# A weight tile's remainder on VectorE instead of GpSimd, in the attention stretches of layers two and three

## What is computed

```python
for i in range(DEPTH_2):
    h = rms_norm_2(x, attn_norm[i])
    proj = h @ w_in_diff[j]            # layer two; w_in_gla[j] in layer three
    ...                                # q, k, v, mem_q from proj
    mix = diff_attention(...)          # gla_attention(...) in layer three
    cross = memory_cross_attention(mem_q, mem, mem_norm[i], w_mem_kv[i], mem_qk_norm[i])
    x = x + jnp.concatenate([mix.astype(x.dtype), cross.astype(x.dtype)], axis=-1) @ w_out[i]
    h = rms_norm_2(x, ffn_norm[i])
    x = x + conv_ffn(h, w_up[i], conv_w[i], conv_b[i], w_down[i])
```

## Time and profile before

| | us |
|---|---|
| median of 3 timed runs | 1799.42 (1798.91 to 1802.1) |
| the profiled execution | 1797.66 |
| its span, first to last instruction | 1795.9 |
| PE busy | 1735.1 (97%) |
| PE weight loads busy | 1403.9 (78%) |
| DVE busy | 945.7 (53%) |
| POOL busy | 746.8 (42%) |
| ACT busy | 477.8 (27%) |

### The profile page before, as it was taken

One profiled execution on the slowest core, in us unless ns is written; L12 is line 12 of the kernel. 1 busy time (PEld: TensorE's weight loads), 2 busy tenths in 40 slices (PEclk: granted clock), 3 DMA queues, 4 the chain that ended last, 5 costly groups with the idle time before them and its releaser, 6 DMA issues.

```text
span 1795.9 us, 28022 instructions
## 1 busy us (share of the span) xinstructions
PE 1735.1 (97%) x11634; PEld 1403.9 (78%) x11634; DVE 945.7 (53%) x1610; ACT 477.8 (27%) x1039; POOL 746.8 (42%) x372
## 2 busy tenths in 40 slices
PE   8999989999899999899999999999999999999999
PEld 7678768887667777777888888877876788888887
DVE  6676245666655376746655551234434466665311
ACT  3111123445232354423222220123121332222100
POOL 3333135200544132237555554553233665555542
PEclk9999999999899999999999999999999999999999
DMA  5222120000234122113223322221112233323332
GB/s 194 83 82 88 44 87 3 3 3 3 89 109 139 46 97 74 59 59 106 96 94 96 103 95 94 95 91 59 59 58 71 74 94 102 97 94 95 104 95 71
DMA packets 43644, 143.95 MB, mean 80 GB/s; under 512 B 5191, under 2 KB 7128, under 8 KB 43390
## 3 DMA queue, kind: packets, MB, share of 16 engines
q1 hardware_dynamic: 43518, 142.15, 24.8%
HBM read 139.50 MB, written 4.08 MB: 80 GB/s over the span
## 4 chain that ended last, share of the span: by engine, by line
PE 66%; DVE 3%; ACT 2%; issue 1%; POOL 0%; DMA 0%; DVEq 0%; SPq 0%; ACTq 0%
PE all_p_bank L214 20%; PE all_p_bank L216 19%; PE all_p_bank L215 19%; PE all_p_bank L2553 1%; PE all_p_bank L2582 1%; PE all_p_bank L2340 1%; PE all_p_bank L2316 1%; PE all_p_bank L2570 0%; PE all_p_bank L2067 0%; PE all_p_bank L3050 0%; PE all_p_bank L3032 0%; PE all_p_bank L3045 0%; PE all_p_bank L2327 0%; POOL b_wlo L195 0%; PE all_p_bank L2516 0%
## 5 line engine op out<-in xcount | busy, mean ns | idle before, releaser
L195 POOL TENSOR_TENSOR b_wlo<-b_raw,b_whi 128x1024 fp32r<-128x1024 f32 x235 | 576.2, 2455 | 748.2 <-DVE b_whi L181 745.6
L214 PE MATMUL all_p_bank<-b_hi,b_whi 128*128 128x512 f32 x1232 | 498.7, 405 | 7.7 <-issue 6.1
L216 PE MATMUL all_p_bank<-b_hi,b_wlo 128*128 128x512 f32 x1232 | 482.8, 392 | 0.0
L215 PE MATMUL all_p_bank<-b_lo,b_whi 128*128 128x512 f32 x1232 | 482.7, 392 | 0.0
L181 DVE CAST b_whi<-b_raw 128x1024 fp32r<-128x1024 f32 x238 | 184.7, 782 | 424.1 <-PE all_p_bank L216 410.3
L214 PEld LDWEIGHTS all_p_bank<-b_hi,b_whi 128*128 128x128 f32 x1232 | 233.0, 189 | 72.4 <-issue 26.1
L216 PEld LDWEIGHTS all_p_bank<-b_hi,b_wlo 128*128 128x128 f32 x1232 | 232.9, 189 | 49.9
L215 PEld LDWEIGHTS all_p_bank<-b_lo,b_whi 128*128 128x128 f32 x1232 | 233.0, 189 | 49.5 <-issue 4.1
L214 PE MATMUL all_p_bank<-f_mhi,b_whi 128*128 128x512 f32 x352 | 136.9, 389 | 0.0
L215 PE MATMUL all_p_bank<-f_mlo,b_whi 128*128 128x512 f32 x352 | 136.9, 389 | 0.0
L216 PE MATMUL all_p_bank<-f_mhi,b_wlo 128*128 128x512 f32 x352 | 136.9, 389 | 0.0
(11 more groups left out here) (459 smaller groups left out, 2566.4 us busy)
## 6 DMA issues: line engine op xcount, KB each, us to landing
b_raw<-in_w_up SPq DMA_DIRECT2D x88, 512.0 KB, 3.5
b_raw<-in_w_down SPq DMA_DIRECT2D x44, 512.0 KB, 3.5
b_raw<-in_w_in SPq DMA_DIRECT2D x32, 512.0 KB, 3.5
b_raw<-in_w_out SPq DMA_DIRECT2D x24, 512.0 KB, 3.6
b_raw<-in_w_gla SPq DMA_DIRECT2D x22, 512.0 KB, 3.5
b_raw<-in_w_diff SPq DMA_DIRECT2D x20, 512.0 KB, 3.5
b_raw<-in_w_mem SPq DMA_DIRECT2D x8, 512.0 KB, 3.6
all_x<-in_x SPq DMA_DIRECT2D x8, 256.0 KB, 5.6
```

The source lines that it names most:

```text
L195: self.nc.gpsimd.tensor_tensor(self.lo[:, n % SLOTS, :], self.raw[:, n % RAWS, :], self.hi[:, n % SLOTS, :].bitcast(F32), ALU.subtract).th ...
L214: nc.tensor.matmul(acc, lhsT=left[0], rhs=right[0], start=first, stop=False)
L215: nc.tensor.matmul(acc, lhsT=left[0], rhs=right[1], start=False, stop=False)
L216: return nc.tensor.matmul(acc, lhsT=left[1], rhs=right[0], start=False, stop=last)
```

## The change

`Ring` gets a list of tile ranges. In a range, `round` makes the remainder on DVE right behind the rounding (`low`), and `rest` on POOL skips the tile. Where a range begins, DVE waits until POOL has made the remainder of the tile in front; where one ends, POOL waits for DVE's last. The ranges are tiles 36 to 75 and 142 to 171: from the last half of layer one's output product to layer two's feed-forward, and layer three's projections and output product. In the feed-forwards POOL makes the remainders as before.

```diff
@@ Ring.__init__
+        self.ranges = []
@@ Ring.round
             self.rounded = n + 1
+            if self.whole(n):
+                if not self.whole(n - 1):
+                    dve.wait_ge(self.s_lo, n)
+                self.low(dve, n)
+
+    def whole(self, n):
+
+        return any(a <= n < b for a, b in self.ranges)
 
     def split(self, dve, n):
 
         self.round(dve, n)
+        self.low(dve, n)
+
+    def low(self, dve, n):
+
         dve.wait_ge(self.s_hi, n + 1)
         self.nc.vector.tensor_tensor(self.lo[:, n % SLOTS, :], self.raw[:, n % RAWS, :],
                                      self.hi[:, n % SLOTS, :].bitcast(F32), ALU.subtract).then_inc(self.s_lo, 1)
@@ Ring.rest
         for n in range(self.rested, min(upto + 1, len(self.tiles), self.limit)):
+            self.rested = n + 1
+            if self.whole(n):
+                continue
+            if self.whole(n - 1):
+                pool.wait_ge(self.s_lo, n)
             pool.wait_ge(self.s_hi, n + 1)
...
-            self.rested = n + 1
@@ upper_layers
+    c.ring.ranges = [(base + 4, low.ff.n_up), (low.ff.down[1].n0 + low.ff.down[1].tiles, high.ff.n_up)]
     run(nc, u.ring, base, plan + plan3, TwoLayers(low, high), Sides(*side, *side3), begin, store)
```

## The result

The changed kernel is slower: 1811.72 us, the median of 4 runs (1810.85 to 1816.08), beside 1799.78 for the kernel before on the same chip. The ratio is 1.0068, 95% interval 1.0054 to 1.0082, so +12 us where the forecast was +3.1 and the range ended at 1808. The profiled execution is the slowest of the four, 1816.08 us. In what follows a ratio is to the kernel before on the same chip, with its 95% interval in brackets; the kernel before had medians of 1799.4 to 1800.1 us on the chips used.

The account below looks back on a forecast made before the run. The prediction took TensorE (busy 1735.1 of 1795.9 us) to bound the kernel; waits added and removed at single places summed to +3.1 us, clock 0, on the timed median 1799.42, giving 1802.5 us, range 1796.5 to 1808.

Parts of the forecast that it names:

- B: Layer two, 629.7 us: two roundings ahead of the first L2641, which PE's next scores wait for; +2.4 us.
- H: Layer two, 747 us: PE's 2.99 us wait for stretched L2616 shrinks despite two remainders; net -1.6 us.
- C: Layer two, 648.9 us: one rounding ahead of L2641, L2553 starting 0.2 after it; +1.1, two like places +0.7 together.
- V: Layer three, 1376.7 us: rounding directly ahead of the last evacuation, L2809, for which PE already waits; +1.3 us.
- A: 508 us: four remainders ahead of the fourth addition to x, which L1898 on PE needs; +1.6, then -0.3 at L2032.
- L: 814 us: an unstretched rounding heads the additions PE waits for before the feed-forward; -0.6 us.
- Elsewhere idle DVE time behind the rounding takes it: Layer two's attention, other places of the L2641 pattern: idle DVE time absorbs the added remainder, so no cost was counted.
- The clash: DVE's new subtraction could be stretched by POOL's remaining work; three clashes at stalls would add 6 us, left out.
- The clock: Half-speed clock pieces behind stalls: one made, one shrunk, set against each other as 0, bounds -3.4 to +3.4 us.
- Rival 1: Layer two's attention: more stalls than counted, about nine roundings without idle DVE time behind; 1807 us, chance 0.26.
- Rival 3: All is hidden: DVE has a third of its time free, gains and costs stay off the path; 1799.5, chance 0.12.
- Rival 2: Faster: the freed interface outweighs DVE's longer queue, 629.7 and 508 us covered by other PE work; 1795.4, chance 0.14.

Follow-up runs that it names:

- e11: The change with the remainders of tiles 54 and 55 given back to POOL: 1807.33 us, ratio 1.0046 to the kernel before.
- e3: The change with eight tiles (54, 55, 57, 148, 149, 155, 167, 170) given back to POOL: 1794.89 us, ratio 0.9983 to the kernel before.
- e12: The change with the remainders of tiles 148 and 149 given back to POOL: 1805.42 us, ratio 1.0029 to the kernel before.
- e1: The change with only its first range, tiles 36 to 75 (layer two), on DVE: 1805.27 us, ratio 1.0029 to the kernel before.
- e9: The change with each DVE remainder two program steps later and ten more tiles given back to POOL, 60 left on DVE: 1793.77 us, ratio 0.9971.
- e10: The change with sixteen tiles given back to POOL, 54 left on DVE directly behind their roundings: 1793.26 us, ratio 0.9971 to the kernel before.
- e7: The change with all 70 remainders on DVE, each two program steps behind its rounding: 1800.35 us, ratio 1.0 to the kernel before.
- e6: The kernel before plus an extra DVE reduction ahead of seven roundings, its result buffer placed so no address moves: 1817.11 us, ratio 1.0100.
- e8: The change with only tile 54's remainder given back to POOL: 1814.59 us, ratio 1.0077 to the kernel before.
- e4: The kernel before plus an extra DVE reduction ahead of seven roundings, with a result buffer that shifted other buffers: 1830.88 us, ratio 1.0182.
- e2: The change with only its second range, tiles 142 to 171 (layer three), on DVE: 1806.30 us, ratio 1.0032 to the kernel before.
- e5: The kernel before plus one unused 32-byte-per-partition buffer behind the ring's tiles, no instruction added: 1818.13 us, ratio 1.0097.

## Why the prediction was wrong, point by point

- **What is moved, and its price: right.** 70 remainders, 1.22 us each at the median, 1.9 us from rounding to rounding (632.78 - 630.91 = 1.87 in the fence at B). The stretched instructions shrank: L2633 takes 0.68 to 0.69 us in all six, H's 2.82 among them.
- **B, C, V: right.** Displacement +2.4 for +2.4, +1.1 for +1.1, +1.3 for +1.3. C's two likes gave 0.9 of wait for 0.7.
- **A: too high in the profiled run.** +0.5 for +1.6. In e11's trace PE waits 1.42 us there and the step is 1.6 more than before's, as forecast, so it varies with the execution. L2032's like at L2049 gave 0.3 as said.
- **H, L, O: right.** -1.75 for -1.6, -0.6 for -0.6, -1.2 for -1.1. **U: less,** -0.3 for -0.8. **I: right in sum,** +0.4 for +0.4, but made up otherwise: the wait for L2637 went from 1.10 to 2.58 us at 761.9, the next from 0.09 to 1.07, and the one behind it fell from 3.01 to 0.87. L's halved stretch at 823 us went too, yet gave nothing: PE came 1.6 us earlier to the feed-forward's first products and waited there instead, from 837 to 843 us, for the norm's remainders (L290 on DVE).
- **"Elsewhere idle DVE time behind the rounding takes it": a step that failed.** It asked whether DVE had time left before its next instruction. At the silu's place DVE did have it, but as a wait for ACT, which waited for the evacuation that the remainder now delays. At N the evacuation stands directly behind the roundings, and what waits for it is ACT and then PE. The slack has to be followed along the chain DVE, ACT, PE. Missed: +2.2 us of wait at N and +0.9 at 1290; e3 has both gone with the tiles, e12 that at N. With the clash's +0.9 at 1426, the +0.5 at 837 and small gains elsewhere, the places that the forecast didn't name add up to +3.3 us of idle time, and those that it named to some +1.9 instead of +3.1, the shortfall chiefly at A: +5.2 in all.
- **The clash: left out, and it was there once on the path.** The Trainium skill (GPSIMD Engine Reference, 1. Specifications) says that GpSimd shares its SBUF interfaces with VectorE and contends with VectorE instructions that have two SBUF inputs. The trace agrees, in both directions. Where POOL's L2976 had started first, DVE's remainder took 2.19 us instead of 1.22; where DVE's had started first, L2976 took 2.24 where the same one took 1.28 before:

```profile
1370.81 1.81 POOL L2976 TENSOR_TENSOR l_mlo<-l3r_x,l_mhi 128x512 fp32r<-128x512 f32 x1 [0.54 <-ACT l_mhi L3125]
...
1371.50 2.19 DVE L201 TENSOR_TENSOR b_wlo<-b_raw,b_whi 128x1024 fp32r<-128x1024 f32 x1
...
1424.01 1.23 DVE L201 TENSOR_TENSOR b_wlo<-b_raw,b_whi 128x1024 fp32r<-128x1024 f32 x1
...
1424.12 2.24 POOL L2976 TENSOR_TENSOR l_mlo<-l3r_x,l_mhi 128x512 fp32r<-128x512 f32 x1 [3.81 <-ACT l_mhi L3125]
...
1426.41 0.50 PE L231 MATMUL all_p_bank<-l_mhi,b_whi 128*128 128x512 f32 x1 [1.04 <-POOL l_mlo L2976]
```

PE waited 1.04 us for it at 1426 and 0.09 before. One clash on the path, 1 us; my three for 6 us would have been too many and too dear.
- **The clock: the step that failed by most.** "I set one against the other: 0, with bounds of two pieces." The net was 17.1 us more at half clock, which cost 8.1 us, far outside the bounds of 3.4, against idle time of +5.2. The step counted one new stall behind which a halved stretch could come, though the prediction itself had B, V and C as new or longer waits; all three have one in the changed kernel, and so have N (6.8 us) and the silu's place, which it had missed. It let gains at H and L cancel them: the region of H and I has three halved stretches before and three after, and L's was worth nothing. e11 shows the wait and its halved stretch at B going together, 2.5 and 1.5 us.
- **The rivals.** Rival 1 had the direction and named slack too small, but in layer two's attention, where e1 found +5.2 us; layer three cost as much. Its own sign, PE's busy share of 620 to 770 us falling by over 5 us, didn't come: 136.45 for 137.08. Its time of 1807 is a slip, too: it names one or two clock pieces, but its sum ends with -0.5 and has no term for them. At the prediction's own price of up to 1.7 us each they would have led to some 1809 to 1811. Rival 3, all hidden, fell with the result. Rival 2 comes near e9 and e10 in time, not in mechanism: they are fast because tiles were given back, not because A and B were covered.

What stays open: why the same 2 us stall brings half clock in the change and none in e12, and why an unchanged wait of 1.50 us (1341.9 in the change, 1328.3 before) has a halved stretch behind it in the change and none before; and a 0.9 us wait for a DMA of the gate's weights at 1203.9 in e7 and 1201.5 in e9, which the others don't have.

## What to carry to other kernels

When work is put into an in-order queue, list what stands behind it up to the next instruction on the bound engine, through every engine between, and give the slack of that whole chain, not the idle time of the next instruction. Moving work to a half-idle engine is good or bad by place: here 8 tiles of 70 made the difference between 0.7% slower and 0.2% faster (the latter with an interval that reaches no change). In this kernel a new stall of TensorE of over 2 us cost 1.6 to 2.2 times its length where half clock followed it (4.0 us at B and 5.6 at N for 2.5 each); elsewhere nothing followed. And put an experiment's scratch buffer where it moves no other.

## What the runs showed of the hardware

- In layers two and three the clock is halved in stretches of 3.4 or 6.8 us. The 17.1 us more of it in the change cost 8.1 us, 0.47 per microsecond (e6: 8.9 for 20.5). At B 2.36 us of wait were followed by 3.4 us in the change, 3.32 and 3.33 by 6.8 in e8 and e6 (3.34 by 3.4 in e4), and no wait by none. It isn't a function of one stall: at the silu's place a wait of 2.05 or 2.06 us was followed by 3.4 in the change and in e2, by 6.8 in e8 and e11, and by none in e12; and 0.64 at N in e2 was followed by 3.4.
- With the normed input's hi and lo 32 bytes higher, the matmuls that read them step at 0.233 us instead of 0.226, at full granted clock; those that read unshifted buffers don't change (e5, ratio 1.0097). Other offsets weren't tried.
- When DVE's 128x1024 subtraction and POOL's 128x512 one ran beside each other, the one that had started second took about 1 us longer: DVE's 2.19 for 1.22 us at 1371.5 and 1379.5, POOL's 2.24 for 1.28 at 1424.1 in the change, and 2.18 and 2.23 at 1399.3 and 1408.1 in e7.
